# Streaming encoder step: the sample's rows prepared before GpSimd's W_out halves, z of chunk 0 turned among its out pieces, the sample's W_out pieces fetched weight group by weight group

## What is computed

```python
h = _rmsnorm(x, norm_g)
u = jnp.einsum('btd,de->bte', h, w_in)
a_b, a_c, a_x, a_g, b_v, b_a, b_g, c_u, c_g, x_q, x_g = jnp.split(u, N_SPLITS, axis=-1)
v = a_c * a_x
y_a = a_b * _dwconv(vpad, conv_a_w) * jax.nn.silu(a_g)          # 3 taps
glu = b_v * jax.nn.sigmoid(b_a)
z = _layernorm(_dwconv(gpad, conv_b_w) + conv_b_bias, ...)      # 31 taps
y_b = jax.nn.silu(z) * jax.nn.silu(b_g)
y_c = mixed * pool_scale * jax.nn.silu(c_g)                     # trailing means 2/4/8/16, minus c_u
y_x = o * jax.nn.silu(x_g)                                      # 4-head attention into 256 tokens
y = jnp.concatenate([y_a, y_b, y_c, y_x], axis=-1)
return x + jnp.einsum('bte,ed->btd', y, w_out), new_a, new_b, new_p
```

## Time and profile before

| | |
|---|---|
| median of three runs | 1479.5 us |
| the profiled execution, device time | 1481.47 us |
| its span, first to last instruction | 1479.7 us |
| granted TensorE clock over the span | 0.993 |
| TensorE matmul busy | 1431.6 us, 97% |
| VectorE busy | 1179.9 us, 80% |
| ScalarE busy | 560.7 us, 38% |
| GpSimd busy | 219.6 us, 15% |
| DMA | 280.88 MB, mean 190 GB/s |

### The profile page before, as it was taken

How to read it: one execution, slowest core, us unless ns; L and a number is a source line. 1 busy time by engine, 2 the same in 40 slices (tenths; PEclk the granted TensorE clock), 3 DMA queues, 4 the chain that set the end, 5 groups by cost and what they waited for, 6 DMA issues and landing times.

```text
span 1479.7 us, 32641 instructions
## 1 busy us (share of the span) xinstructions
PE 1431.6 (97%) x11766; PEld 1227.3 (83%) x11766; DVE 1179.9 (80%) x3084; ACT 560.7 (38%) x1237; POOL 219.6 (15%) x180
## 2 busy tenths in 40 slices
PE   5989999999999999999999999999999999999986
PEld 4777888888888888888888888888888888888864
DVE  6997596977959596896959698695969779595985
ACT  6874243333324342343324233332433333242432
POOL 0151011111101111111111111110111111011110
PEclk9999999999999999999999999999999999999999
DMA  9976445564463556446354655535455644635662
GB/s 266 270 257 212 177 160 185 199 221 176 126 249 121 203 182 224 184 153 252 92 214 168 213 198 178 219 108 223 165 185 198 217 180 124 249 123 203 210 219 89
DMA packets 127522, 280.88 MB, mean 190 GB/s; under 512 B 12297, under 2 KB 69309, under 8 KB 127485
## 3 DMA queue, kind: packets, MB, share of 16 engines
q1 hardware_dynamic: 127485, 280.40, 55.1%
HBM read 221.86 MB, written 58.49 MB: 189 GB/s over the span
## 4 chain that ended last, share of the span: by engine, by line
PE 88%; DVE 4%; DMA 2%; issue 2%; ACT 2%; POOL 0%; SPq 0%; POOLq 0%; ACTq 0%; DVEq 0%
PE u L612 20%; PE u L614 20%; PE u L613 20%; PE sps L612 5%; PE sps L613 4%; PE sps L614 4%; PE qps L612 4%; PE qps L613 4%; PE qps L614 4%; DMA ring<-wo_split 2%; PE ops L721 2%; PE sps L865 1%; DVE z L1613 1%; DVE w_hl L1594 1%; DVE prow L1640 0%
## 5 line engine op out<-in xcount | busy, mean ns | idle before, releaser
L612 PE MATMUL u<-h_hi,w_hl 128*128 128x256 f16 x2816 | 770.4, 274 | 2.4 <-ACT gate L1040 2.4
L614 PE MATMUL u<-h_hi,w_hl 128*128 128x256 f16 x2816 | 769.5, 273 | 0.0
L613 PE MATMUL u<-h_lo,w_hl 128*128 128x256 f16 x2816 | 769.5, 273 | 0.0
L1613 DVE SCALAR_TENSOR_TENSOR z<-glu,cst,z 128x256 f32<-128x256 f32 x960 | 414.7, 503 | 0.5
L612 PEld LDWEIGHTS u<-h_hi,w_hl 128*128 128x128 f16 x2816 | 276.5, 98 | 46.4 <-issue 7.6
L614 PEld LDWEIGHTS u<-h_hi,w_hl 128*128 128x128 f16 x2816 | 276.2, 98 | 32.7
L613 PEld LDWEIGHTS u<-h_lo,w_hl 128*128 128x128 f16 x2816 | 276.4, 98 | 32.2 <-issue 0.7
L1040 ACT ACTIVATE gate<-u,inv 128x256 f32<-128x256 f32 x192 | 79.7, 466 | 114.8 <-PE u L614 114.6
L2117 POOL TENSOR_TENSOR sa<-cu 128x540 f32<-128x540 f32 x16 | 30.1, 1880 | 545.7 <-ACT cu L1040 481.5
L612 PE MATMUL qps<-ring,y_hi 128*128 128x512 f32 x256 | 102.3, 400 | 4.9 <-DMA ring<-wo_split 4.9
L612 PE MATMUL sps<-ring,y_hi 128*128 128x512 f32 x256 | 101.4, 396 | 0.0
(11 more groups left out here) (323 smaller groups left out, 1986.2 us busy)
## 6 DMA issues: line engine op xcount, KB each, us to landing
ring<-wo_split SPq DMA_DIRECT2D x248, 512.0 KB, 8.0
ob<-in_x_prompt SPq DMA_DIRECT2D x34, 512.0 KB, 4.2
probs_turned<-probs SPq DMA_DIRECT2D x128, 128.0 KB, 2.4
pt<-probs_turned SPq DMA_DIRECT2D x32, 512.0 KB, 3.4
out<-ob SPq DMA_DIRECT2D x32, 512.0 KB, 3.1
rows_turned<-rows SPq DMA_DIRECT2D x112, 128.0 KB, 2.4
w_hl<-in_w_in SPq DMA_DIRECT2D x20, 512.0 KB, 7.4
wo_split<-ring SPq DMA_DIRECT2D x16, 512.0 KB, 5.0
```

The costliest lines, as they stand in the source:

```text
L612: nc.tensor.matmul(out, a_hi, b_hi, start=first, stop=False)
L613: nc.tensor.matmul(out, a_hi, b_lo, start=False, stop=False)
L614: return nc.tensor.matmul(out, a_lo, b_hi, start=False, stop=last)
L1613: ins = nc.vector.scalar_tensor_tensor(z[:, c, 0:n], glu[:, c, k:k + n], w, z[:, c, 0:n], ALU.mult, ALU.add)
```

## The change

Four things are moved, and no arithmetic changes.

1. The sample's rows. SP loads x_sample behind weight group 4 instead of behind group 10. ScalarE squares it behind `pool_weights_hi`, VectorE makes its root (now by itself, ten instructions on 64 rows) and its scaling behind `w_scale(5)`, TensorE turns it behind weight sum 6, and the two halves `hs` are made behind `w_high(11)` and `w_low(11)`. `early_rms` and `late_rms` go; x's two next tiles get one root of 16 instructions behind `z_norm` (`both_rms`). `keys_t(0)`, which writes the same bank, waits for `hs`.
2. Chunk 0's z. `z_rows` stands behind W_out piece 3 instead of ahead of sample groups 9 and 10, `z_back` behind piece 8 instead of 5, `attend(0, N, 1)` ahead of groups 9 and 10, and VectorE takes `yx_out` ahead of `z_stats`. One more sample group stands ahead of b_g.
3. The sample's late W_out pieces are issued in four pairs, each when a weight group has been used (a_g, b_g, c_g, x_g), the last pair behind the ring's piece 13.
4. The order in the last chunk: ScalarE's a_g gates ahead of the sample's `probs_hi`; VectorE's `va` and conv A of the sample ahead of `z_stats`, more of its taps ahead of `yx_out`, none between the additions; TensorE's `z_back` of the sample behind 6 of its pieces instead of 10.

```diff
             load_split(4)
+            sp.dma_start(xs_rows, x_sample[0]).then_inc(res_s.sem, 16)
             for g in range(5, NG - 2):
                 load_split(g)
...
             load_split(NG - 1)
-            sp.dma_start(xs_rows, x_sample[0]).then_inc(res_s.sem, 16)
...
+            def late_pieces(pair):
+                sp.wait_ge(u_ready.sem, slot(LAST, ORDER[7 + pair])[0])
+                for b in range(2 * pair, 2 * pair + 2):
+                    sp.dma_start(late[b].bitcast(F32), wo_split[b]).then_inc(wo_late.sem, 16)
...
                 sp.dma_start(xs, x_sample[0]).then_inc(res_s.sem, 16)
+                late_pieces(0)
                 probs_across(LAST, 1, N)
+                late_pieces(1)
                 probs_across(CHUNKS, 0, SAMPLE)
-                sp.wait_ge(u_ready.sem, slot(LAST, "x_g")[0])
-                for b in range(RING):
-                    sp.dma_start(late[b].bitcast(F32), wo_split[b]).then_inc(wo_late.sem, 16)
-                for q in range(RING, PIECES):
+                late_pieces(2)
+                for q in range(RING, PIECES - 2):
+                    ring_load(LAST, q)
+                late_pieces(3)
+                for q in range(PIECES - 2, PIECES):
                     ring_load(LAST, q)
...
                 if k == 0:
                     pe.wait_ge(kv_ok.sem, 2)
+                    pe.wait_ge(xs_step.sem, XS_LO)
...
                 weight_sums(6)
+                sample_transposes()
                 memory_product(5)
...
                 scores(0, N, 1)
-                sample_transposes()
-                for g in range(3):
+                for g in range(4):
                     sample_project(g)
                 project(0, N, "b_g")
                 weight_sums(10)
-                for g in range(3, 7):
+                for g in range(4, 7):
                     sample_project(g)
...
                 sample_project(8)
-                z_rows(0, N)
+                attend(0, N, 1)
                 for g in range(9, 11):
                     sample_project(g)
-                attend(0, N, 1)
                 out_begin(0, N)
-                out_pieces(0, N, 0, Z_AT)
+                out_pieces(0, N, 0, 4)
+                z_rows(0, N)
+                out_pieces(0, N, 4, 9)
                 z_back(0, N)
-                out_pieces(0, N, Z_AT, PIECES - 2 * CT)
+                out_pieces(0, N, 9, PIECES - 2 * CT)
...
                 sample_pieces(0, 6)
+                z_back(i, n)
+                sample_pieces(6, 8)
                 states_out(1, SAMPLE)
-                sample_pieces(6, 10)
-                z_back(i, n)
-                sample_pieces(10, PIECES)
+                sample_pieces(8, PIECES)
...
                 pool_weights_hi()
+                sample_squares()
...
                 exps(i, n, 0)
                 probs_hi(LAST, N, 1)
-                probs_hi(i, n, 0)
                 scaled_out(LAST, N, "a_g", gate[:, 2, :, 0:N], ACT.Silu, ag_ok)
                 scaled_out(i, n, "a_g", S.gate[:, 2], ACT.Silu, ag_ok)
+                probs_hi(i, n, 0)
...
+            def both_rms(j):
+                dve.wait_ge(x_sq.sem, j + 2)
+                dve.wait_ge(x_scaled.sem, j)
+                rsqrt(x_v, 0, RSQRT * j, X_SQ, X_V, X_SH, X_Y, 1.0 / D, skip=2 * RSQRT - (4 + 4 * NEWTON))
+
+            def sample_rms():
                 dve.wait_ge(xs_step.sem, XS_SQ)
...
+                rsqrt(m_v, 0, 0, *(v[0:SAMPLE, 0:1] for v in (M_SQ, M_V, M_W, M_Y)), 1.0 / D)
...
                 w_scale(5)
+                sample_rms()
+                sample_scale()
                 taps(0, N, 10, 11)
...
                 w_low(11)
+                sample_lo()
...
-                early_rms(nxt[0][0])
-                sample_scale()
...
+                yx_out(0, N)
                 z_stats(0, N)
-                yx_out(0, N)
                 z_norm(0, N)
-                late_rms(*nxt[1])
-                early_scale(*nxt[0])
+                both_rms(nxt[0][0])
+                rows_scale(*nxt[0], after=2)
...
                 pool_diff(i, n)
+                va_out(i, n)
+                conv_a_taps(i, n)
                 z_stats(LAST, N)
                 yx_out(LAST, N)
                 z_norm(LAST, N)
                 d_low(i, n)
-                va_out(i, n)
-                conv_a_taps(i, n)
                 ab_out(i, n)
                 ya_out(i, n)
+                taps_free(i)
+                taps(i, n, 0, 4)
                 yb_out(LAST, N)
-                taps_free(i)
-                taps(i, n, 0, 14)
+                taps(i, n, 4, 29)
                 yx_out(i, n)
-                taps(i, n, 14, 28)
+                taps(i, n, 29, TB)
                 add_half(LAST, N, 0)
-                taps(i, n, 28, TB)
                 add_half(LAST, N, 1)
```

More of the change, by code:

```diff
@@ L132, in encoder_program @@
             xs_rows = raw_stage[0:SAMPLE, 0:D]
+            early_junk = raw_stage[:, 0:D // 2].bitcast(BF16)
         y_lo = sb("y_lo", [P, KT, N], F32R)
@@ L1053, in squares @@
                     act.wait_ge(o_sq.sem, o_sq.at(i, 0))
-                nc.scalar.activation(junk[0:m, :], rows[0:m, :], ACT.Square,
+                out = early_junk if type(j) is int and j == 4 else junk
+                nc.scalar.activation(out[0:m, :], rows[0:m, :], ACT.Square,
                                      accum_out=into[0:m, t:t + 1]).then_inc(x_sq.sem, 1)
@@ L1297, in first_chunk @@
                 w_high(11)
+                sample_hi()
                 w_square(18)
@@ L1304, in first_chunk @@
                 w_high(14)
-                squares(*nxt[0], into=M_SQ)
-                sample_squares()
+                squares(*nxt[0])
                 piece_hi(0)
@@ L1321, in first_chunk @@
                 w_high(17)
-                sample_hi()
                 piece_hi(8)
```

36 lines of the change are left out of this document (5 added, 31 removed).

## The result

The changed kernel takes 1473.87 us (median of six executions, 1471.61 to 1477.27) beside 1481.06 for the kernel before (six, 1478.83 to 1484.36): ratio 0.9947 [0.9929, 0.9965]. A second series on another chip gave 0.9957 [0.9942, 0.9971]. That is 6.4 to 7.9 us, where the prediction said 12.0: the direction and the range held, the size did not. 1473.87 lies just inside the range's 1474.0; the second series' median, 1475.01 beside 1481.86 for the kernel before, lies outside it as a time, but as a change it is inside, since the range meant 5.5 to 16.5 us off a median of 1479.5. The profiled execution took 1472.62 us (span 1470.8).

The account below looks back on a forecast made before the run. TensorE is busy throughout the loop, so gains lie in its waits in chunk 0 (3.0 us) and the end (9.0): 12.0 off the profiled 1481.5 gives 1469.5, or 1467.5 us for the median; range 1463.0 to 1474.0.

Parts of the forecast that it names:

- Placing of the sample's rows: Chunk 0: x_sample lands at about 40.4, ScalarE squares at 41.6 without waiting, rows are scaled at 57.7 us.
- the fourth rival: Chunk 0: x_sample lands behind all ten weight loads, delaying ScalarE, VectorE and TensorE; up to 1487.5 us; chance 0.04.
- The clock behind the new wait: Chunk 0: TensorE's 3.3 us wait before the moved transposes, 54.4 to 57.7, costs 0.5 us through a lower clock.
- The full charge of 1.6 us: Chunk 0: upper bound for slow clock behind the moved transposes' wait; by it chunk 0 would be worth 1.9 us.
- 14.2 us from turn to `mix`, none of it shortened: Chunk 0: VectorE's probabilities turn ends at 106.6 to 108.2, not 110.9, so `mix` comes 3.5 us earlier.
- the 3.6 us shift: Chunk 0: ScalarE's keys_values and GpSimd's windows move some 3.6 us later with TensorE's wait before the transposes.
- The first rival: Chunk 0 gives nothing, `mix` stays put: 1470.5 us, or 1472 with a 1.6 us clock charge; chance 0.15.
- It fell to 0.50 there before, and I leave that as it is: Chunk 0: the clock around `mix` falls to 0.50 as before, so no gain or loss is counted there.
- a rival of its own: Third rival, chunk 0: the clock doesn't fall around `mix`, saving 2.5 us and some tenths: 1464.5 us; chance 0.08.
- The end: Last chunk with the sample: shorter TensorE waits and less slow clock give 9.0 us, bounds 6.5 and 9.8.
- the second rival: The end is bound by VectorE, its sample work 3 us later than placed: end gives 6 us, 1470.5; chance 0.08.
- 4.4 + 1.6 us: The end: earlier W_out loads remove TensorE's 4.4 us wait before piece 8 and 1.6 us of slow clock.

Follow-up runs that it names:

- the rows alone: Kernel before plus only the sample's rows moved (part 1), z of chunk 0 and last chunk as before: 1482.72 us, ratio 1.0012.
- half kept: Changed kernel writing out only the high half of each W_out piece in chunk 0, read twice later (wrong values): 1492.34 us, ratio 1.0082.
- The two kernels with filled waits: Changed kernel, transposes behind memory product 5, sample groups 8 and 9 before head pair 0's attention: 1469.17 us; same with VectorE's ya and yx earlier: 1468.59 us.

## Why the prediction was right and wrong

**Placing of the sample's rows: right.** The scaling started at 56.37 and the transposes at 57.70, as put; the x_sample load was in time, ScalarE's square at 41.38 shows no wait, so the fourth rival is out.

**The clock behind the new wait: wrong, and by a misreading.** "I take 0.5", on the ground that a 3.59 us wait at 20.8 had left 1.00. Seven profiles with this wait, of 2.8 to 4.3 us, all show a fall; it cost 1.7 us in the profile of the changed kernel (0.24 of five us at 0.76, and 0.5 in the stretch before) and near 3 with the rows alone. The wait at 20.8 had not left full speed either, though its row says 1.00. In the kernel before, the products behind it have the length that the same products have in the changed kernel at the slow clock, 0.42 us, and from 28.8 on that of the full clock, 0.27:

```profile
24.97 0.42 PE L613 MATMUL u<-h_lo,w_hl 128*128 128x256 f16 x1
...
28.81 0.27 PE L613 MATMUL u<-h_lo,w_hl 128*128 128x256 f16 x1
```

and in the changed kernel, behind the new wait:

```profile
61.49 0.42 PE L622 MATMUL u<-h_lo,w_hl 128*128 128x256 f16 x1
...
62.61 0.27 PE L622 MATMUL u<-h_lo,w_hl 128*128 128x256 f16 x1
```

So TensorE ran slow behind the wait at 20.8, at 1.2 GHz by the length of its products. The trace holds no record of the clock before 28.8 us, and the view prints 1.00 where it has none. The weight sums ahead of that wait are slow too (0.57 us at 19.77, against 0.36 for the same two products at 54.18), so the row can't show what the wait did. The Trainium skill (TensorE: Matmul & The Clock Gate, What's actually happening) has half speed as the default, and these products at the start agree. The full charge of 1.6 us, which I had priced by that rule and set aside, was the nearer, and what I set it aside for was no evidence.

**"14.2 us from turn to `mix`, none of it shortened": this step failed.** Everything from the turn to `mix` was charged to the chain that ended last before. But ScalarE had only 4.84 us of slack where the exponentials wait, and its own work ahead of that point moves with TensorE's shift. It was free at 111.0 before (115.84 less 4.84); with the 3.6 us shift I had forecast that is 114.6, which leaves 1.2 us at `mix` and not 3.5. With the clock's loss and the pieces' loads (waits of 1.67 and 1.25 us for pieces 13 and 14) the shift there was 4.5, and nothing was left. The turn did come earlier, but ended at 110.0 instead of 106.6 to 108.2. The first rival had this outcome, at 0.15; with its clock charge it gave 1472 for the median, 2 us under what was measured.

**"It fell to 0.50 there before, and I leave that as it is": right in the main.** The fall around `mix` is there in five of the same seven profiles (0.50 to 0.66) and missing in two, the first of the changed kernel and half kept. At 0.50 for five us it costs 2.5 us, and so a rival of its own was the wrong shape for it: it is not a property of the changed kernel but of the execution.

**The end: 9.0 forecast, 8.1 by the traces.** The waits for ring, the a_g gate, the sample's z and its y_lo went as put. z_rows of the sample is at 1449.4 for 1448.7, but 0.8 of that comes from ahead of the last chunk: counted from the first mark of the end it is 7.1 us earlier than before, where I had put 8.5, and the other 1.0 of the 8.1 comes behind it. What was missing is the second y_lo wait of 0.74 us, before the pieces of X: yx of chunk 15 stands behind the sample's conv A and z_stats, a move that I had costed at nothing. The placing of VectorE's 50 taps held, and the second rival (VectorE bound) did not come.

**Why it went: wrong, with a sum that came near by luck.** I gave 4.4 + 1.6 us to the early loads. They do remove that wait, and by themselves give 5.9, but the order removes it too. Beside the order the early loads add nothing, and the order without them gives all 8.1. I had seen that the pieces would wait for y_lo in place of the gate (1.4 us), but not that such waits also give the loads time. Pricing the order alone, with the late loads kept, would have shown the ring's wait shrinking in it.

**The sum.** Chunk 0 3.0 forecast, about 0 found; the end 9.0 forecast, 8.1 found in the traces and 6.4 to 7.9 in the times. Of the 6.4 us between the forecast median of 1467.5 and 1473.87, 1.6 come from the base: three executions of the kernel before gave 1479.5, six gave 1481.06.

## What to carry to other kernels

Before a row of the granted clock is taken as evidence, hold it against the length of like products in the same stretch. When a wait is moved earlier, price each engine's slack at the next meeting point, not only the chain that ended last there: the idle time ahead of an instruction (the bracket) is all that a shift may use before it arrives. For a wait with two remedies in one change, look for how each moves the issue and the use of the same transfer, since their gains may be the same microseconds. And where TensorE must wait, put its own later work there: it is paid twice, in the wait and in the clock behind it.

## What the runs showed of the hardware

Thirty extra products paid for themselves: with them the granted clock from 55 to 65 us is 1.00 instead of 0.90 and 0.76 (or 0.99 and 0.67), and the first scores come 0.5 us earlier. The ratios, 0.9933 with them and 0.9947 and 0.9957 without, point the same way, with intervals that overlap.

The same orders around both places give other clocks in other executions: 0.76, 0.67, 0.64, 0.53, 0.57, 0.81 and 0.73 from 60 to 65 us, and 1.00 in two, 0.50 to 0.66 in five from 125 to 130. The first product of chunk 1 moves by some 2 us with the clock of the later stretch. The two kernels with filled waits have the same three stops of 0.3, 0.6 and 0.9 us between 80 and 84 us; behind them the clock is 1.00 in one and 0.75 in the other (85 to 90 us).

VectorE's probs_lo (four instructions) took 1.70 us in five profiles where GpSimd's piece halves ran beside it for 0.4 us of that time, and 2.94 to 4.14 us in six where they ran beside it for 1.7 to 3.6 us. The difference, up to 2.4 us, is as large as what many of the edits moved.
